# Stick-breaking attention on one core: products in two 64-row tiles throughout, and projection groups as a stream of halves

## The chip, the cores and the metric

The kernel runs on one core of a Trainium2 chip. The metric is the device time of one execution in microseconds, as the median of several runs. The input is one sequence of 2048 tokens with 1024 columns, all in float32.

## The reference

With DEPTH = 1 only the first kind of layer runs, the stick-breaking attention. Cut to what matters:

```python
h = rmsnorm(x, a_norm)
q, k, v, g = split(h @ w_in, 4)              # 16 heads of 64
for each head, t, s < t:
    z = (q[t] . k[s]) / 8
    log_beta, log_rem = log_sigmoid(z), log_sigmoid(-z)
    w[t, s] = exp(log_beta + sum of log_rem[t, j] over s < j < t)
o[t] = sum over s of w[t, s] * v[s]
out = rmsnorm(x + (o * silu(g)) @ w_out, final_norm)
```

## The kernel before

The tokens are reversed on the host, so that the product over the keys between s and t becomes a running product along a row. The kernel never forms the weights w. ScalarE makes sigmoid(-z) of the scores (`stick`, L1161), VectorE multiplies it up along the row with a scan (`scan`, L1381), and since w is the difference of two neighbouring running products, the kernel multiplies the running product with differences of v (`dv_head`) instead.

Every product of two float32 matrices is made from three products of reduced float32 numbers, high part by high part, high by low and low by high. So each operand has a high part (a copy on ScalarE) and a low part (a subtraction on VectorE or GpSimd).

**Stages.** First v for all tokens (L817), then ten groups of the q, k and gate projection. Then the attention, with the rest of the projection spread through it, and at the end the output projection (L995), the residual and the last norm.

**Attention.** A step is 128 queries of one head against a chunk of 512 keys. Four steps are one slot, with 10 slots a head (4 on the diagonal, whose steps have 512, 384, 256 and 128 columns, and 6 full ones of 512 columns), 160 slots in all. In slot s TensorE makes, in the order in which it is written out:

- scores of slot s + 2 (L886): 12 products with 64 rows of contraction. Steps alternate between the upper and lower half of the array's rows, so two run beside one another.
- turns of slot s (L919, or L932): transposes of the running products, each as two 64-row halves into PSUM. ScalarE copies a pair of steps out as the high part (`hi`, L1166), and VectorE takes the low part (`lo`, L1385).
- one projection group (`project`, L864): 24 products of 256 columns on all 128 rows, in some slots two groups. A group is emptied by `made_high` on ScalarE and `made_low` on VectorE (L1365, L1367) and stored.
- weighings of slot s (`weigh`, L964 and L965): 8 products on 128 rows into the bank o_ps. At the end of a chunk of queries ScalarE empties that bank (`empty`, L1172) and the parts are stored.

The order of each engine is written out in a loop over the slots. `SLOT_GROUPS` says which slot has which groups, `LOAD_W`, `HI_W` and the `PAIR_` tables say at which step weights and differences of v are loaded and split. The turned parts have two places in PSUM, four banks in all (`turn_ps`), the scores three banks, whose free ones are lent to the groups.

## Time and profile before

| | us |
|---|---|
| median of 3 runs | 1605.23 |
| lowest and highest | 1601.46, 1605.66 |
| the profiled execution's own time | 1601.61 |
| its span, first to last instruction | 1599.9 |
| TensorE busy | 1577.8 |
| VectorE busy | 1281.8 |
| ScalarE busy | 848.4 |
| GpSimd busy | 423.5 |

A busy time is the union of an engine's instructions. Products on TensorE overlap, so its busy share says only that it had work; what a product costs is the distance between the starts of two that follow each other. The attention lasts from about 233 us to 1428 us.

### The profile page before, as it was taken

Reading aid. Unit: us, or ns where it says so; the run is one execution under the profiler, and the core shown is the slowest. Engines: PE = TensorE matmul, PEld = TensorE weight load, DVE = VectorE, ACT = ScalarE, POOL = GpSimd, SP = SyncE. Lnnn points to the kernel's source line nnn. Section 1 sums busy time; section 2 is a strip of 40 time slices with the busy share of each in tenths; the row PEclk is TensorE's granted clock in tenths of the full one; section 3 lists DMA queues with packets and bytes.
Section 4 is the critical chain, followed back from the end, with each engine's and each line's share of the span. In section 5 each row is a group of like instructions: output and inputs, shape, how many; then the busy total and the mean of one; then the engine's idle time right before and its main releaser. Section 6 shows DMA issues by size and latency. Waiting matters only on the chain.

```text
span 1599.9 us, 34375 instructions
## 1 busy us (share of the span) xinstructions
PE 1577.8 (99%) x13762; PEld 1382.1 (86%) x13762; DVE 1281.8 (80%) x1525; ACT 848.4 (53%) x1558; POOL 423.5 (26%) x520
## 2 busy tenths in 40 slices
PE   9999999999999999999999999999999999999998
PEld 7888888888898888888888888888888988778887
DVE  5445439898889898898989898889899888967883
ACT  6535335555555556556556565565556555752221
POOL 0022034223323243323432433233223432000000
PEclk9999999999999999999999999999999999999999
DMA  9868654443434252435343443424243433879632
GB/s 304 268 182 271 203 159 126 125 124 99 137 102 136 74 158 78 139 86 146 110 115 115 120 117 96 138 91 143 77 142 103 131 110 110 326 254 342 206 106 79
DMA packets 205887, 237.82 MB, mean 149 GB/s; under 512 B 54560, under 2 KB 162080, under 8 KB 205728
## 3 DMA queue, kind: packets, MB, share of 16 engines
q1 hardware_dynamic: 113344, 160.30, 32.7%
q10 hardware_dynamic: 92384, 75.33, 15.3%
q8 instruction: 109, 1.79, 0.5%
q14 instruction: 50, 0.41, 0.1%
HBM read 155.78 MB, written 79.76 MB: 147 GB/s over the span
## 4 chain that ended last, share of the span: by engine, by line
PE 84%; DVE 9%; ACT 3%; issue 2%; DMA 1%; SPq 0%; DVEq 0%; ACTq 0%
PE z_ps L864 29%; PE z_ps L886 12%; PE o_ps L965 6%; PE turn_ps L919 6%; PE o_ps L964 6%; DVE u L1381 5%; PE turn_ps L995 5%; PE z_ps L817 5%; PE z_ps L995 4%; DVE r_turned_lo L1385 3%; PE o_ps L817 3%; PE turn_ps L817 3%; PE turn_ps L864 1%; PE turn_ps L886 1%; PE o_ps L995 1%
## 5 line engine op out<-in xcount | busy, mean ns | idle before, releaser
L1381 DVE TENSOR_TENSOR_SCAN u<-u,u 128x512 f32<-128x512 f32 x384 | 500.0, 1337 | 0.0
L1161 ACT ACTIVATE u<-z_ps 128x512 f32<-128x512 f32 (+3 forms) x593 | 288.1, 541 | 302.2 <-PE z_ps L886 301.7
L864 PE MATMUL z_ps<-hT_hi,w_hi 128*128 128x256 f32 x1472 | 432.5, 294 | 2.9 <-ACT u L1161 2.1
L1385 DVE TENSOR_TENSOR r_turned_lo<-turn_ps,r_turned_hi 128x1024 fp32r<-128x1024 f32 (+1 forms) x320 | 324.0, 1053 | 129.5 <-ACT r_turned_hi L1166 128.3
L864 PE MATMUL z_ps<-hT_hi,w_lo 128*128 128x256 f32 x1472 | 416.0, 283 | 0.0
L864 PE MATMUL z_ps<-hT_lo,w_hi 128*128 128x256 f32 x1472 | 415.9, 283 | 0.0
L864 PEld LDWEIGHTS z_ps<-hT_hi,w_hi 128*128 128x128 f32 x1472 | 280.6, 191 | 28.9 <-issue 17.5
L864 PEld LDWEIGHTS z_ps<-hT_lo,w_hi 128*128 128x128 f32 x1472 | 281.3, 191 | 0.0
L864 PEld LDWEIGHTS z_ps<-hT_hi,w_lo 128*128 128x128 f32 x1472 | 281.2, 191 | 0.0
L1166 ACT ACTIVATE r_turned_hi<-turn_ps 128x1024 fp32r<-128x1024 f32 (+1 forms) x320 | 270.5, 905 | 6.6 <-PE turn_ps L919 6.6
L759 POOL TENSOR_SCALAR w_raw<-w_raw,a_norm_col 128x128 f32<-128x128 f32 x192 | 171.4, 909 | 241.5 <-DMA w_raw<-in_w_qkg 241.5
L964 PE MATMUL o_ps<-r_turned_hi,dv_head 128*128 128x512 f32 (+3 forms) x640 | 226.9, 359 | 0.0
L965 PE MATMUL o_ps<-r_turned_lo,dv_head 128*128 128x512 f32 (+3 forms) x640 | 223.9, 365 | 0.0
L1381 DVE TENSOR_TENSOR_SCAN u<-u,unbroken 128x512 f32<-128x512 f32 (+3 forms) x256 | 205.6, 843 | 2.7 <-ACT u L1161 2.7
L767 POOL TENSOR_TENSOR w_lo<-w_raw,w_hi 128x128 fp32r<-128x128 f32 x192 | 137.2, 745 | 215.1 <-ACT w_hi L1115 215.1
L886 PE MATMUL z_ps<-k_hi_twice,q_hi 64*128 64x512 f32 (+3 forms) x593 | 160.4, 441 | 8.9 <-issue 2.9
L919 PEld LDWEIGHTS turn_ps<-ident,u 64*128 64x128 f32 x4070 | 154.4, 139 | 13.2 <-DVE made L1367 0.5
L919 PE MATMUL turn_ps<-ident,u 64*128 64x64 f32 x4070 | 156.7, 223 | 0.0
L781 POOL TENSOR_TENSOR dv_head<-v_here,dv_head 128x256 fp32r<-128x256 f32 x64 | 53.8, 841 | 305.2 <-ACT dv_head L1109 305.2
L964 PEld LDWEIGHTS o_ps<-r_turned_hi,dv_head 128*128 128x128 f32 x640 | 120.8, 189 | 15.9 <-DVE r_turned_lo L1385 1.2
L965 PEld LDWEIGHTS o_ps<-r_turned_lo,dv_head 128*128 128x128 f32 x640 | 120.9, 189 | 15.5
L886 PE MATMUL z_ps<-k_hi_twice,q_lo 64*128 64x512 f32 (+3 forms) x593 | 133.3, 371 | 0.0
(157 smaller groups left out, 2220.9 us busy)
## 6 DMA issues: line engine op xcount, KB each, us to landing
qk_hi_cols<-made ACTq DMA_DIRECT2D x128, 128.0 KB, 2.3
qk_lo_cols<-made ACTq DMA_DIRECT2D x128, 128.0 KB, 2.3
k_hi_twice<-qk_hi_cols SPq DMA_DIRECT2D x128, 128.0 KB, 3.4
k_lo_twice<-qk_lo_cols SPq DMA_DIRECT2D x128, 128.0 KB, 3.7
x_T<-in_xT SPq DMA_DIRECT2D x29, 512.0 KB, 6.3
w_raw<-in_w_qkg SPq DMA_DIRECT2D x24, 512.0 KB, 3.8
x_rows<-in_x SPq DMA_DIRECT2D x16, 512.0 KB, 5.2
v_rows<-v_stage ACTq DMA_DIRECT2D x32, 256.0 KB
```

What stands on the lines that cost most here:

```text
L759: last = nc.gpsimd.tensor_scalar(w_raw[t % 2][:, k, :], w_raw[t % 2][:, k, :], norm_col[:, k:k + 1], None, ALU.mult)
L817: last = nc.tensor.matmul(v_ps[v % len(v_ps)][:], a[:, c, k, tok], b[:, k, :], start=(k == 0 and n == 0), stop=(k == KT - 1 and n == 2))
L864: last = nc.tensor.matmul(bank_of(g)[:, 0:GW], a[t % 2][:, k, :], b[:, c // 2, k, cols], start=(n == 0), stop=(n == QPM - 1))
L886: last = nc.tensor.matmul(score_bank(step), a[c % 2][rows, tau], b[rows, sig], start=(n == 0), stop=(n == 2))
L919: last = nc.tensor.transpose(turn_ps[p % 2][:, half, at:at + HALF], u_t[m // CB % RU][t][rows, r * P - lo:(r + 1) * P - lo], ident[rows, r ...
L964: nc.tensor.matmul(o_ps[:, 0:w], weights, rt_hi[p % 2][:, here], start=begin, stop=False)
L965: last = nc.tensor.matmul(o_ps[:, 0:w], weights, rt_lo[p % 2][:, here], start=False, stop=end)
L995: last = nc.tensor.matmul(y_banks(n)[f][:], a[t % RG][:, k, tok], b[:, k, f * CH:(f + 1) * CH], start=(m == 0), stop=(m == QPM - 1))
L1161: nc.scalar.activation(u_t[(m // CB) % RU][r][:, 0:w], score_bank(m), ACT.Sigmoid, scale=-Z_SCALE).then_inc(s_u, 1)
L1166: nc.scalar.activation(by_halves(rt_hi[p % 2][:], p), turned(p), ACT.Copy).then_inc(s_hi, 1)
L1381: nc.vector.tensor_tensor_scan(u, u, other, start, ALU.mult, op).then_inc(s_r, 1)
L1385: nc.vector.tensor_tensor(by_halves(rt_lo[p % 2][:], p), turned(p), by_halves(as_f32(rt_hi[p % 2][:]), p), ALU.subtract).then_inc(s_lo, 1)
```

## The change

All products of the attention work in 64-row tiles now. A weighing is split in two, over the upper and the lower 64 rows, and runs in one half of the array beside scores of a later slot in the other half (`weigh_beside`). The lower and the upper part of one pair of steps go one after the other into the same bank, with semaphores between them. The projection groups become a stream of halves: each of the 24 products of a group is an upper and a lower one, and the lower ones are at least 30 behind the upper ones, so that a group's lower half begins after its upper one has ended. `QUOTA` sets how many halves of each kind a half slot gets (12 on the diagonal, 15 else). Where a weighing takes more columns than the scores beside it, or fewer, group halves are put on the half with less.

The turned parts have one place in PSUM (two banks), and the turns of a pair of steps wait for the low part of the pair before. Scores have two banks, groups three. VectorE makes one scan, then the low part, then the other scan of a half slot; ScalarE's order is by half slots too. Separate forms of the turns beside scores (`turns_beside_scores`) are gone.

```diff
-SLOT_GROUPS = groups_of_slots()
+AHEAD = {-2: (BEFORE, BEFORE + 1), -1: (BEFORE + 2, BEFORE + 3)}
+FIRST = BEFORE + 4
+BEHIND = 30
+QUOTA = {True: 12, False: 15}
+STREAM = (NG - FIRST) * QPM
...
+def limits():
+    upto = [0]
+    for h in range(2 * NU):
+        _, c, j, _ = STEPS[CB * (h // 2)]
+        upto.append(min(upto[-1] + QUOTA[c == j], STREAM + BEHIND))
+    return upto
...
-        turn_ps = [ctx.enter_context(nc.psum_tensor(f"turn_ps{n}", [P, 2, CH], F32)) for n in range(2)]
-        t_ps = [turn_ps[n // 2][:, n % 2, :] for n in range(4)]
+        turn_ps = ctx.enter_context(nc.psum_tensor("turn_ps", [P, 2, CH], F32))
+        t_ps = [turn_ps[:, 0, :], turn_ps[:, 1, :], pb("group_ps0"), pb("group_ps1")]
+        g_ps = [z_ps[2], t_ps[2], t_ps[3]]
...
                 def turns(p):
 
+                    if p:
+                        pe.wait_ge(s_lo, p)
...
+                def group_half(low):
+                    i = made_so_far[low]
+                    made_so_far[low] += 1
+                    g, n = FIRST + i // QPM, i % QPM
+                    t, c = GROUPS[g]
+                    cols = slice(c % 2 * GW, (c % 2 + 1) * GW)
+                    if n == 0 and low:
+                        pe.wait_ge(s_gu, g - FIRST + 1)
+                    if n == 0 and not low:
+                        pe.wait_ge(s_plo, g - 2)
+                        if g == FIRST_G[t]:
+                            pe.wait_ge(s_wlo, t + 1)
+                    rows = slice(low * HALF, (low + 1) * HALF)
+                    k, (a, b) = n // 3, ((w_hi, hT_hi), (w_hi, hT_lo), (w_lo, hT_hi))[n % 3]
+                    last = nc.tensor.matmul(bank_of(g)[:, 0:GW], a[t % 2][rows, k, :], b[rows, c // 2, k, cols],
+                                            start=(n == 0 and not low), stop=(n == QPM - 1 and low == 1))
...
+                def left(h, low):
+                    limit = UPTO[h + 1] - BEHIND if low else UPTO[h + 1]
+                    return max(0, min(limit, STREAM) - made_so_far[low])
+
+                def group_pairs(h, share):
+                    both = min(left(h, 0), left(h, 1)) // share
+                    for _ in range(both):
+                        group_half(0)
+                        group_half(1)
+                    if share == 1:
+                        for low in range(2):
+                            for _ in range(left(h, low)):
+                                group_half(low)
+
+                def weigh_half(m, low, part):
...
+                    first = begin and not low and part == 0
+                    if first and NC * h + c:
+                        pe.wait_ge(s_ost, NC * h + c)
+                    rows = slice(low * HALF, (low + 1) * HALF)
+                    here = slice(blocks_before(m) * P, blocks_before(m) * P + w)
+                    turned_part = (rt_hi, rt_lo)[part]
+                    last = nc.tensor.matmul(o_ps[:, 0:w], dv_head[rows, j * CB + sigma_block(m), :], turned_part[p % 2][rows, here],
+                                            start=first, stop=(end and not low and part == 1))
...
+                def weigh_beside(p, low, m, h):
+                    weighed = inside(p // 2)
+                    scored = m < NS
+                    if weighed:
+                        pe.wait_ge(s_lo, p + 1)
+                        if p % 2 == 0 and low:
+                            pe.wait_ge(s_wu, p // 2 + 1)
+                        if p % 2 and not low:
+                            pe.wait_ge(s_wl, p // 2 + 1)
+                    for i in range(2 * PAIR):
+                        if weighed:
+                            weigh_half(PAIR * p + i // 2, low, i % 2)
+                        if scored and i < 3:
+                            score(m, i)
+                    width = 2 * (turn_width(PAIR * p) + turn_width(PAIR * p + 1)) if weighed else 0
+                    spare = width - (3 * (CH - score_cols(m)) if scored else 0)
+                    idle = low if spare < 0 else 1 - low
+                    for _ in range(min(abs(spare) // GW, left(h, idle))):
+                        group_half(idle)
...
+                for s in range(NU):
+                    ahead = CB * (s + LEAD)
+                    pe.wait_ge(s_r, CB * s + CB)
+                    turns(2 * s)
+                    weigh_beside(2 * s - 1, 1, ahead, 2 * s)
+                    group_pairs(2 * s, 2)
+                    weigh_beside(2 * s - 1, 0, ahead + 1, 2 * s)
+                    group_pairs(2 * s, 1)
+                    if s >= OUT_SLOT:
+                        put_out((s - OUT_SLOT) * QPM, (s - OUT_SLOT) * QPM + QPM // 2)
+                    turns(2 * s + 1)
+                    weigh_beside(2 * s, 0, ahead + 2, 2 * s + 1)
+                    group_pairs(2 * s + 1, 2)
+                    weigh_beside(2 * s, 1, ahead + 3, 2 * s + 1)
+                    group_pairs(2 * s + 1, 1)
...
@@ scalar
+                    for part in range(2):
+                        h, first = 2 * s + part, CB * s + PAIR * part
+                        for g in finished(h - 1):
+                            made_high(g)
+                            store_high(g)
+                        if inside(s):
+                            hi(h)
+                        for g in finished(h - 1):
+                            store_low(g)
+                        if inside(s + LEAD):
+                            stick(first + LEAD_SCORES)
+                            stick(first + LEAD_SCORES + 1)
...
+                        if ended is not None and part == 0:
+                            empty(ended)
+                        if ended is not None and part == 1:
+                            store_o(ended)
...
@@ vector
+                    for part in range(2):
+                        h, first = 2 * s + part, CB * s + PAIR * part
+                        for g in finished(h - 1):
+                            made_low(g)
+                        for m in range(first + LEAD_SCORES - PAIR, first + LEAD_SCORES):
+                            if 0 <= m < NS:
+                                scan(m)
+                            if inside(s) and m % PAIR == 0:
+                                lo(h)
```

## Rows read from the trace of the kernel before

**Rows 1.** The page: busy times, and the chain that ended last by engine.
```profile
PE 1577.8 (99%) x13762; PEld 1382.1 (86%) x13762; DVE 1281.8 (80%) x1525; ACT 848.4 (53%) x1558; POOL 423.5 (26%) x520
PE 84%; DVE 9%; ACT 3%; issue 2%; DMA 1%; SPq 0%; DVEq 0%; ACTq 0%
```

**Rows 2.** The chain of waits in order of time: start us, us, what; the double slots.
```profile
459.17 5.96 PE z_ps L864 x48
...
1350.85 5.95 PE z_ps L864 x48
```

**Rows 3.** Busy PE, PEld, DVE, ACT, POOL in these heads; granted clock, DMA share, GB/s.
```profile
459.17:1350.85 891.68, 887.91 (x8907) 789.61 (x8905) 795.34 (x856) 517.67 (x969) 309.64 (x368) 1.00 0.39 114
```

**Rows 4.** Timeline of TensorE, one full slot: start us, us, what, count.
```profile
702.19 0.39 PE L964 MATMUL o_ps<-r_turned_hi,dv_head 128*128 128x512 f32 x1
702.42 0.39 PE L965 MATMUL o_ps<-r_turned_lo,dv_head 128*128 128x512 f32 x1
702.74 0.50 PE L886 MATMUL z_ps<-k_hi_twice,q_hi 64*128 64x512 f32 x2
703.07 0.40 PE L886 MATMUL z_ps<-k_hi_twice,q_lo 64*128 64x512 f32 x2
...
703.54 1.16 PE L919 MATMUL turn_ps<-ident,u 64*128 64x64 f32 x32
704.51 0.48 PE L886 MATMUL z_ps<-k_hi_twice,q_hi 64*128 64x512 f32 x2
704.83 0.39 PE L886 MATMUL z_ps<-k_hi_twice,q_lo 64*128 64x512 f32 x2
...
705.39 0.39 PE L864 MATMUL z_ps<-hT_hi,w_hi 128*128 128x256 f32 x1
705.61 0.28 PE L864 MATMUL z_ps<-hT_lo,w_hi 128*128 128x256 f32 x1
705.73 0.28 PE L864 MATMUL z_ps<-hT_hi,w_lo 128*128 128x256 f32 x1
...
710.30 0.50 PE L886 MATMUL z_ps<-k_hi_twice,q_hi 64*128 64x512 f32 x2
```

**Rows 5.** The waits: engine and line, waited for, us in total, times, longest us.
```profile
PEld z_ps L886 <- issue: 43.7, 107, 3.3
```

**Rows 6.** Timeline of TensorE in diagonal scores of 256 and 128 columns.
```profile
696.12 0.54 PE L886 MATMUL z_ps<-k_hi_twice,q_hi 64*128 64x256 f32 x2
696.34 0.18 PEld L886 LDWEIGHTS z_ps<-k_hi_twice,q_hi 64*128 64x128 f32 x1 [0.20 <-PE z_ps L886]
696.34 0.43 PE L886 MATMUL z_ps<-k_hi_twice,q_lo 64*128 64x256 f32 x2
696.45 0.29 PEld L886 LDWEIGHTS z_ps<-k_lo_twice,q_hi 64*128 64x128 f32 x2
696.57 0.32 PE L886 MATMUL z_ps<-k_lo_twice,q_hi 64*128 64x256 f32 x2
```

**Rows 7.** Timeline of TensorE in diagonal weighings.
```profile
687.10 0.33 PE L964 MATMUL o_ps<-r_turned_hi,dv_head 128*128 128x384 f32 x1
687.27 0.34 PE L965 MATMUL o_ps<-r_turned_lo,dv_head 128*128 128x384 f32 x1
```

**Rows 8.** ScalarE: two instructions of its timeline, then groups by line (count, busy us, mean ns).
```profile
703.74 0.60 ACT L1161 ACTIVATE u<-z_ps 128x512 f32<-128x512 f32 x1 [2.35 <-PE z_ps L886]
704.23 0.59 ACT L1161 ACTIVATE u<-z_ps 128x512 f32<-128x512 f32 x1
L1166 ACT ACTIVATE r_turned_hi<-turn_ps 128x1024 fp32r<-128x1024 f32 x144 | 140.2, 1032 | 0.0
L1172 ACT ACTIVATE o_stage<-o_ps 128x512 f32<-128x512 f32 x48 | 30.1, 627 | 0.0
```

**Rows 9.** VectorE: the scans' spread (ns min/median/max), and the low parts by line.
```profile
L1381 DVE TENSOR_TENSOR_SCAN u<-u,u x384: 1248/1274/1821, 225.7 to 1406.6; 128x512 f32<-128x512 f32 x192
L1385 DVE TENSOR_TENSOR r_turned_lo<-turn_ps,r_turned_hi 128x1024 fp32r<-128x1024 f32 x144 | 169.2, 1216 | 75.0 <-ACT r_turned_hi L1166 74.1
```

More of the change, by code:

```diff
@@ L491, in lows_stored @@
                 eng.wait_ge(s_gst[parity], low_stores(g, parity))
[L493 to L498 removed]
         def score_bank(m):
[L502 to L507 removed]
+            return z_ps[m % 2][:, 0:CH - score_cols(m)]
         def bank_of(g):
@@ L866, in project, with score @@
                     last.then_inc(s_p, 1)
-                def scores(m):
-                    r = m % CB
-                    steps = (m + 1, m) if diagonal(m // CB) and r == 0 else (m, m + 1)
-                    for n in range(3):
-                        for step in steps:
-                            if diagonal(m // CB) and n == 0 and step % CB == CB - 1:
-                                pe.wait_ge(s_z, CB * (m // CB) + 1)
-                            score(step, n)
-                def score(step, n):
-                    _, c, j, r = STEPS[step]
+                def score(m, n):
+                    h, c, j, r = STEPS[m]
+                    if n == 0:
+                        if m >= 2:
+                            pe.wait_ge(s_u, m - 1)
+                        if r == 0 and c == 0:
+                            pe.wait_ge(s_k[j], 64 * (h + 1))
+                        if r == 0 and j == c:
+                            pe.wait_ge(s_q[c % 2], 64 * (2 * h + c // 2 + 1))
                     a, b = ((q_hi, k_hi), (q_lo, k_hi), (q_hi, k_lo))[n]
@@ L957, in weigh @@
-                    if begin and NC * h + c:
+                    first = begin and not low and part == 0
+                    if first and NC * h + c:
                         pe.wait_ge(s_ost, NC * h + c)
-                    p = m // PAIR
-                    if m % PAIR == 0:
-                        pe.wait_ge(s_lo, p + 1)
-                    here = slice(blocks_before(m) * P, blocks_before(m) * P + w)
-                    weights = dv_head[:, j * CB + sigma_block(m), :]
-                    nc.tensor.matmul(o_ps[:, 0:w], weights, rt_hi[p % 2][:, here], start=begin, stop=False)
@@ L965, in weigh @@
-                    last = nc.tensor.matmul(o_ps[:, 0:w], weights, rt_lo[p % 2][:, here], start=False, stop=end)
-                    if end:
-                        last.then_inc(s_o, 1)
-                    elif j == c and r == CB - 1:
-                        last.then_inc(s_dvused, 1)
+                    rows = slice(low * HALF, (low + 1) * HALF)
[3 more added lines that the diff above has]
+                                            start=first, stop=(end and not low and part == 1))
@@ new lines, in weigh_half @@
+                    if part == 1 and m % PAIR == 1:
+                        if p % 2 == 0 and not low:
+                            last.then_inc(s_wu, 1)
+                        elif p % 2 and low:
+                            last.then_inc(s_wl, 1)
+                        elif p % 2 and end:
+                            last.then_inc(s_o, 1)
+                        elif p % 2 and j == c:
+                            last.then_inc(s_dvused, 1)
+                def weigh_beside(p, low, m, h):
+                    weighed = inside(p // 2)
+                    scored = m < NS
+                    if weighed:
+                        pe.wait_ge(s_lo, p + 1)
+                        if p % 2 == 0 and low:
[12 more added lines that the diff above has]
+                        group_half(idle)
@@ L1277, in _ @@
-                    if inside(s + LEAD):
-                        stick(CB * (s + LEAD) + 2)
-                        stick(CB * (s + LEAD) + 3)
-                    if ended is not None:
-                        store_o(ended)
-                    for m in range(CB * s, CB * s + CB):
-                        if m in PAIR_HI:
-                            dv_hi(*PAIR_HI[m])
-                    for n, g in enumerate(SLOT_GROUPS.get(s, [])):
-                        if n:
-                            store_low(g - 1)
-                        made_high(g)
-                        store_high(g)
```

206 lines of the change are left out of this document (67 added, 139 removed).

## The prediction

> **What bounds the kernel now.** I read the page first: TensorE is busy 99% of the span, VectorE 80%, and the chain that ended last lies 84% on TensorE [rows 1]. The reader should not stop there, because a busy TensorE can be one that runs the wrong things slowly. So next the chain of waits in order of time, which gives the rhythm: two groups of projection in one slot (48 products in one row) recur once a head, and from 459.17 to 1350.85 are 12 heads, 74.3 us each [rows 2]. They hold 3 further double slots, so 11.25 groups (270 products of 256 columns) a head. The busy table over the same stretch says VectorE works 795 of 892 us, 66.3 us a head, and that TensorE has its full clock of 2.4 GHz (1.00) throughout [rows 3]. That is how much room there is: a head can't go below about 66 us, and TensorE must be the one that shortens it.
>
> Then the timeline of TensorE over one slot, whose starts tell what each thing costs [rows 4]. A slot whose weighings and scores are both full takes 7.56 us (702.74 to 710.30). Starts lie 0.12 us apart for a 256-column product on all 128 rows, 0.23 for a 512-column weighing, 0.235 for a pair of 512-column scores in the two row halves (two in 0.47, 703.07 to 703.54), and 0.030 for one 64-column turn (32 in 0.97 us, the halves taking turns, 0.061 a pair). Where the kind of tile changes there are steps longer than these: the last weighing before the scores takes 0.32 (0.09 over), the first scores 0.33 (0.10 over), the last scores before the group 0.33 (0.56 for two, 704.83 to 705.39, 0.09 over), the first product of the group 0.22 (0.10). The waits name them: 107 weight loads of scores come after idle time that no semaphore ended, some 0.35 us each as the weight loader counts it [rows 5]. The first scores after the turns take 0.32 too, with no change of tile: the wider weight load isn't hidden behind a 64-column product. That is 0.083 over.
>
> **The change, part by part.**
> *Switches removed.* With weighings and groups in 64-row tiles, a slot has no change of kind: minus 0.38 us of the slot above.
> *Exposed loads added.* Each of the two batches of turns is now followed by weighings and scores, so 0.083 twice a slot, 20 a head: 1.7 us.
> *Turns* stay: 32 in a full slot and 20 in a diagonal one, 6 and 4 slots a head, 272 x 0.0303 = 8.2 us.
> *Weighings beside scores.* Each of the 40 calls a head puts four weighings in one half and three scores in the other, then the spare column count in 256-column halves of groups on the half that has less. They are written W S W S W S W, then the group halves. What counts is whether a product can pass one written before it that waits for the other half. Rows 6 speak on that: at 696.12 a 256-column score is followed in its half by one that waits for nothing but its own half, free at 696.24, yet it starts at 696.34, when the other half's score written before it has been released by its semaphore (weight load, 0.20 idle). So program order holds across the halves, and I count with it: a product starts when its half is free and the one before it has started. The spare halves then start only with the fourth weighing. With 0.232 for 512 columns (between 0.229 and 0.235), 0.172 for 384 [rows 7], 0.11 for 128 (its load, which takes the 0.11 between two load starts [rows 6]) and 0.122 for 256, a call takes: full weighings beside scores of 512, 384, 256, 128 columns 0.94, 1.06, 1.31, 1.43 us (16, 2, 3, 3 of them; the last is 3 x 0.232 + 6 x 0.122); the first pair of a diagonal slot 0.82, 1.12, 1.25 (6, 1, 1, beside 512, 256, 128); its second pair 0.94 beside 512 (0.464 until the fourth weighing, 0.11, and three halves) and 0.59 beside 384 (6, 2). Sum 39.5 us a head. In them run 106 group halves, worth 53 full products.
> *Groups as halves.* 270 - 53 = 217 pairs a head. The trace has no pair of 256-column halves. Below it is bounded by the full product, 0.120 [rows 4], and by the one half seen alone in its lane, 0.12 from its load at 696.45 to its start at 696.57 [rows 6]. Above, I take 0.130: the aligned pair of 512-column scores costs 6 ns more than a full product, which I double. Nearest is the 0.12 plus a part of the 6 ns: 0.122. 217 x 0.122 = 26.5 us.
> Together 39.5 + 26.5 + 8.2 + 1.7 = 75.9 us against 74.3: plus 1.5 to 1.6, 25 us over 16 heads. The unmixed slot gains (0.97 + 0.17 + 4 x 0.94 + 20 x 0.122 = 7.3 for 24 products' worth, against 7.56), and the slots where full weighings meet diagonal scores, or diagonal ones meet full scores, give back more.
> On this order stands a rule of the Trainium skill (TensorE: Matmul & The Clock Gate, "The mechanism" in Part 3): products start in program order, whatever their tile, and only weight loads are pulled ahead. It speaks against the change, and the trace agrees with its 0.20 us of idle. The page TensorEngine Tiling (Array Packing), "Key Properties", has the opposite pull: a change of tiling mode drains the engine; by that alone the change would take 0.38 us off each of 160 slots, 61 us in all.
> *The end of a chunk.* The first weighing of a chunk waits for ScalarE to empty o_ps (L1172), and now only the end of one half slot lies between. From the start of the last score of that half slot: 0.39 until its end, 0.04 until ScalarE starts, 0.49 to its next start, 0.63 for the emptying [rows 8], 0.05 to release: 1.6 us. TensorE meanwhile has 0.47 of the call left, five pairs (0.61), six turns (0.18) and the exposed load: 1.3. Behind the waiting weight load stands everything, scores included. 0.3 us, 4 a head, 64 in all: 19 us. Bounds 0 (emptying first seen by TensorE just in time) and 0.5, 32 us. Before, a slot's scores, turns and group (5.6 us) covered it.
> *One turned bank instead of two.* Turns of one half slot wait for the low part of the last. After the turns: 0.2 to ScalarE, 1.03 for the high part, 1.22 for the low one [rows 8, 9], 2.5 us, inside a half slot of 3.6 to 4.1 us. VectorE puts one scan (1.34) ahead of the low part and one behind: 1.34 + 1.22 + 1.34, less 0.08 of overlap each (the next starts so much before the end), and 0.32 for a group in five of eight: 3.9 in a full half slot of TensorE's 4.0. I cost this at nothing: single long scans (up to 1.82) fit into the leeway of over 1 us that the turns' loop has. Without that leeway a long scan costs its 0.5 us, and the cost is rival C's.
> *The stream and its end.* Quotas of 15 and 12 pairs a half slot are 276 a head, 6 more than before, so the 4272 pairs run out in slot 155 instead of 157. Slots 156 and 157 have no group, 4.4 and 3.6 us on TensorE against 7.3 and 4.5 of scans and low parts: 4 us idle. Bounds 0 (the scans had run ahead) and 8. Groups' stores, high parts and weights keep their number; a group's bank is needed 18 pairs after its end, over a half slot, in which its low part is made at the head of VectorE's queue. SP's and POOL's orders keep their steps.
> Sum: 25 + 19 + 4 = 48 us slower than the profiled execution's own 1601.6: 1649 us. That execution stands 3.6 us below the median of 1605.2 and 0.15 above the lowest, so the sum may fall 2 to 3 us short of a median.
>
> **The rivals.**
> A. *The halves slip past each other.* If a group half may start while a weighing written before it waits, a call takes the longer of its two halves' sums: 35.9 instead of 39.5, the head 72.3, minus 2.0 x 16 = 32, and with 19 + 4: 1592, faster; with pairs at 0.120 and no chunk wait 1562. For it: neighbours in opposite halves start within 4 ns. Against it: rows 6. It decides from 1.4 us a head saved.
> B. *Feeding.* A pair is four instructions in 0.12 us. The turns show that rate, 32 in a batch [rows 4], which a queue may hold; over 892 us only 8907 products started, one in 0.10 us [rows 3], and the changed kernel wants about 120 in 8 us. If a product's load and start took 0.075 us when sustained, a pair would be 0.15: 270 x 0.028 = 7.6 a head, 1649 + 121 = 1770. For it: nothing stalls so in the trace. Against: batches at twice that rate.
> C. *VectorE becomes the bound* in full half slots, 3.9 against 4.0. If one in four of the 12 a head loses 0.3 us, that is 0.9 a head, 14 us: 1663 with the forecast (within its range), 1606 with A, no change. For it: 66.3 us a head and scans of 1.82 [rows 3, 9]; against it: the average head leaves it 9 us.
> D. *The chunks' ends wait for nothing*, because the turns before them are late anyway: 1649 - 19 = 1630, at the forecast's low end.
>
> **How the numbers follow.** Forecast with its pitches and waits between their bounds (1622 to 1691: pairs at 0.130 add 42) and D within it 0.66; A 0.20; C with A 0.04; B 0.10. Faster by over 0.3% (5 us, what a measurement here can tell): A and half of C, 0.22; within it 0.05; slower 0.73. Cutting off most of B above and a part of A below: 1582 to 1695; the forecast's own range is 1622 to 1691.
>
> **What would show it.** No idle of the weight loads of scores that no semaphore ends (switches gone); weighings 0.23 apart in one half with scores between them; pairs of group halves 0.122 apart; beside scores of 128 columns, the first spare group half starting with the fourth weighing (order holds) or right after the third score (A is right); waits of the first weighing of a chunk on the emptying, 64 of 0.3 us; a head at 77 us with VectorE busy 86% of it. The forecast is wrong if a head is under 74 us, or if the pair takes 0.115 or 0.14.

## The result, and the profile after

The changed kernel takes 1632.74 us (median of 4 runs, 1623.55 to 1634.36) against 1604.99 (4 runs): a ratio of 1.0166 (interval 1.0125 to 1.0207). It is slower. The profiled execution took 1633.79 us with a span of 1632.0, 32.2 us more than the profiled one of before.

The page: busy times, and the chain that ended last, as in [rows 1].
```profile
PE 1571.3 (96%) x19314; PEld 1458.5 (89%) x19314; DVE 1284.4 (79%) x1525; ACT 883.3 (54%) x1558; POOL 419.5 (26%) x520
PE 74%; DVE 7%; ACT 7%; issue 4%; DMA 3%; ACTq 2%; POOL 1%; SPq 1%; DVEq 0%
```
TensorE is busy for less time than before (1571.3 against 1577.8 us) in a longer span, and its share of the last chain falls from 84% to 74%, while ScalarE's rises from 3% to 7%. So the loss is mostly time in which TensorE waits, and ScalarE has a part in it. TensorE's waits over the whole span (line, waited for, us in total, times, longest us) name two; L902 are the turns, L957 the weighings:
```profile
PE turn_ps L902 <- DVE r_turned_lo L1404: 30.1, 50, 1.8
PE o_ps L957 <- ACT o_stage L1190: 16.3, 46, 3.3
```
The row of [rows 5] has no counterpart: the idle of the scores' weight loads at a change of tile is gone. The second wait is the forecast's emptying at the end of a chunk. The first, turns that wait for the low part of the half slot before, the forecast costed at nothing.

Busy PE, PEld, DVE, ACT, POOL by stretch, then granted clock, DMA share and GB/s: the start of the attention, the 12 heads of [rows 3], and the last head.
```profile
233.00:300.00 67.00, 64.67 (x917) 61.95 (x919) 58.62 (x61) 38.36 (x68) 22.85 (x30) 0.95 0.38 114
459.00:1350.00 891.00, 861.13 (x13031) 832.60 (x13028) 784.30 (x844) 536.04 (x956) 305.41 (x367) 1.00 0.40 114
1350.00:1460.00 110.00, 98.50 (x1132) 85.18 (x1129) 86.15 (x102) 68.19 (x132) 2.19 (x3) 0.94 0.67 224
```
In the 12 heads TensorE now idles 30 of 891 us, where it idled 4 of 892 [rows 3]; 29.2 of the 30 are the two waits (18.2 and 11.0 us there). A head, from one last emptying to the next, takes 75.41 us instead of 74.29 (mean of the 3rd to the 14th, called the steady ones), with 276 pairs of group halves in it and not 270. The last head takes 89.2 us instead of 78.3, and the clock falls to 1.2 GHz in it for two stretches of about 7 us each (from 1373.9 and 1435.3 on).

The 32 us, by the times of the first turn and of the last emptyings: the attention begins 3.3 us earlier; the 15 heads before the last take 26.2 more (the 12 steady ones 12 x 1.12 = 13.4; the others 12.8, of which 7.6 in the very first, 3.1 in the second and 2.0 in the 15th); the last head 10.9 more; what follows it 1.8 less.

How the halves run, from TensorE's timeline (start us, us, what, count): first the pairs of group halves at the end of a call.
```profile
764.30 0.33 PE L923 MATMUL group_ps<-hT_hi,w_hi 64*128 64x256 f32 x2
764.42 0.32 PE L923 MATMUL group_ps<-hT_lo,w_hi 64*128 64x256 f32 x2
764.54 0.33 PE L923 MATMUL group_ps<-hT_hi,w_lo 64*128 64x256 f32 x2
764.65 0.33 PE L923 MATMUL group_ps<-hT_hi,w_hi 64*128 64x256 f32 x2
```
Pairs of group halves start 0.12 us apart (0.117 over 764.30 to 764.65): just under the 0.122 of the forecast. Then a call whose diagonal weighings (256, 256, 128 and 128 columns) stand beside scores of 512 columns:
```profile
766.67 0.28 PE L957 MATMUL o_ps<-r_turned_hi,dv_head 64*128 64x256 f32 x1
766.72 0.28 PE L923 MATMUL group_ps<-hT_hi,w_hi 64*128 64x256 f32 x1
766.79 0.28 PE L957 MATMUL o_ps<-r_turned_lo,dv_head 64*128 64x256 f32 x1
766.84 0.39 PE L880 MATMUL z_ps<-k_hi_twice,q_hi 64*128 64x512 f32 x1
766.91 0.22 PE L957 MATMUL o_ps<-r_turned_hi,dv_head 64*128 64x128 f32 x1
766.97 0.27 PE L957 MATMUL o_ps<-r_turned_lo,dv_head 64*128 64x128 f32 x1
767.08 0.33 PE L923 MATMUL group_ps<-hT_lo,w_hi 64*128 64x256 f32 x1
767.08 0.39 PE L880 MATMUL z_ps<-k_hi_twice,q_lo 64*128 64x512 f32 x1
...
767.31 0.39 PE L880 MATMUL z_ps<-k_lo_twice,q_hi 64*128 64x512 f32 x1
```
They are written W S W S W S W. The fourth weighing starts at 766.97, before the second score (767.08) and the third (767.31), both written ahead of it. In all 124 calls of the trace with such weighings beside scores of 512 or 384 columns the fourth weighing starts before a score written ahead of it, by 0.03 to 0.37 us. Products of one half pass products of the other: rival A's mechanism, which the forecast had ruled out.

One of the new waits, on ScalarE's timeline (ACTq rows are DMAs that its queue issues; L1179 brings a score bank over, L1144 is the high part of a finished group, L1184 the high part of the turned halves). The turns of this half slot started at 447.38 and ended by 448.07.
```profile
446.96 0.28 ACT L1179 ACTIVATE u<-z_ps 128x128 f32<-128x128 f32 x1 [0.93 <-PE z_ps L880]
446.97 0.48 ACTq L1196 DMA_DIRECT2D o_hi_cols<-o_stage  x1
447.49 0.62 ACTq L1197 DMA_DIRECT2D o_lo_cols<-o_stage  x1
448.31 0.39 ACT L1144 ACTIVATE made<-z_ps 128x256 fp32r<-128x256 f32 x1 [1.07 <-PE z_ps L923]
448.72 0.32 ACTq L1156 DMA_DIRECT2D qk_hi_cols<-made  x1
449.09 1.03 ACT L1184 ACTIVATE r_turned_hi<-turn_ps 128x1024 fp32r<-128x1024 f32 x1 [0.40 <-ACT made L1144]
```
The high part starts 1.0 us after its turns are done, behind the output's two DMA issues, the group's high part and that group's store. VectorE and then TensorE follow, each late:
```profile
450.15 1.23 DVE L1404 TENSOR_TENSOR r_turned_lo<-turn_ps,r_turned_hi 128x1024 fp32r<-128x1024 f32 x1 [0.40 <-ACT r_turned_hi L1184]
451.43 0.65 PE L902 MATMUL turn_ps<-ident,u 64*128 64x64 f32 x14 [0.40 <-DVE r_turned_lo L1404]
```
VectorE was idle for 0.40 before its low part, so it was not VectorE's amount of work that made this one late. Counted over the trace, 10 of the 50 waits (6.5 of the 30.1 us) are of this kind. In 30 others (18.7 us) ScalarE's lateness takes a longer way: the low part of a finished group stands at the head of VectorE's half slot and, in 29 of them, is what waits for ScalarE; a scan follows, and then the turned low part. One of these, whose turns had ended by 803.8, and for which ScalarE first issued an output store until 803.58 and copied weights from 803.63:
```profile
804.60 0.36 ACT L1142 ACTIVATE made<-z_ps 128x256 f32<-128x256 f32 x1
804.86 1.02 ACT L1184 ACTIVATE r_turned_hi<-turn_ps 128x1024 fp32r<-128x1024 f32 x1
804.99 0.42 DVE L1384 TENSOR_TENSOR made<-z_ps,made 128x256 f32<-128x256 f32 x1 [1.57 <-ACT made L1142]
805.33 1.40 DVE L1400 TENSOR_TENSOR_SCAN u<-u,u 128x512 f32<-128x512 f32 x1
806.66 1.19 DVE L1404 TENSOR_TENSOR r_turned_lo<-turn_ps,r_turned_hi 128x1024 fp32r<-128x1024 f32 x1
807.90 0.71 PE L902 MATMUL turn_ps<-ident,u 64*128 64x64 f32 x16 [1.19 <-DVE r_turned_lo L1404]
```
The high part is done at 805.88 and lies there for 0.8 us. In the last 10 (4.9 us) VectorE did not idle so shortly before.

The waits sit at the same places. Of the 18.2 us in the 891 us, 15.9 (26 of 32 times) are at four of a head's 20 half slots, and all four come one half slot after one for which ScalarE has, ahead of the group and the high part, the two DMA issues of a chunk's output. Without the waits themselves, half of the half slots ahead of a wait last 3.3 to 3.7 us, where the forecast counted with 3.6 to 4.1.

### The profile page after: what moved, and what is told of

It is laid out like the page before. It is cut to its first block, busy times and chain, and to the rows that moved or that the text cites. A ratio compares the mean times of both kernels' runs of the same rounds, so it can differ in the third digit from the quotient of the medians.

```text
span 1632.0 us, 46030 instructions
## 1 busy us (share of the span) xinstructions
PE 1571.3 (96%) x19314; PEld 1458.5 (89%) x19314; DVE 1284.4 (79%) x1525; ACT 883.3 (54%) x1558; POOL 419.5 (26%) x520
## 4 chain that ended last, share of the span: by engine, by line
PE 74%; DVE 7%; ACT 7%; issue 4%; DMA 3%; ACTq 2%; POOL 1%; SPq 1%; DVEq 0%
PE o_ps L957 14%; PE group_ps L923 14%; PE z_ps L880 10%; PE z_ps L923 7%; PE turn_ps L902 7%; PE z_ps L814 5%; PE z_ps L1014 4%; DVE r_turned_lo L1404 4%; DVE u L1400 3%; PE o_ps L814 3%; PE group_ps L814 3%; PE turn_ps L1014 3%; PE group_ps L1014 2%; ACT o_stage L1190 2%; ACT u L1179 2%
## 5 line engine op out<-in xcount | busy, mean ns | idle before, releaser
L957 PE MATMUL o_ps<-r_turned_hi,dv_head 64*128 64x512 f32 (+3 forms) x1280 | 482.4, 381 | 18.0 <-ACT o_stage L1190 16.3
L1179 ACT ACTIVATE u<-z_ps 128x512 f32<-128x512 f32 (+3 forms) x640 | 336.2, 532 | 251.7 <-PE z_ps L880 241.1
L957 PE MATMUL o_ps<-r_turned_lo,dv_head 64*128 64x512 f32 (+3 forms) x1280 | 454.5, 365 | 0.0
L923 PE MATMUL group_ps<-hT_hi,w_hi 64*128 64x256 f32 x1888 | 451.7, 281 | 0.0
L923 PE MATMUL group_ps<-hT_hi,w_lo 64*128 64x256 f32 x1888 | 449.0, 280 | 0.0
L923 PE MATMUL group_ps<-hT_lo,w_hi 64*128 64x256 f32 x1888 | 446.9, 279 | 0.0
L1184 ACT ACTIVATE r_turned_hi<-turn_ps 128x1024 fp32r<-128x1024 f32 (+1 forms) x320 | 287.7, 899 | 185.8 <-PE turn_ps L902 165.5
L923 PEld LDWEIGHTS group_ps<-hT_hi,w_hi 64*128 64x128 f32 x1888 | 318.8, 186 | 3.1
L923 PEld LDWEIGHTS group_ps<-hT_lo,w_hi 64*128 64x128 f32 x1888 | 315.3, 186 | 2.1
L923 PEld LDWEIGHTS group_ps<-hT_hi,w_lo 64*128 64x128 f32 x1888 | 314.5, 186 | 1.0
L923 PE MATMUL z_ps<-hT_hi,w_hi 64*128 64x256 f32 x960 | 269.9, 281 | 0.0
L923 PE MATMUL z_ps<-hT_hi,w_lo 64*128 64x256 f32 x960 | 269.1, 280 | 0.0
L957 PEld LDWEIGHTS o_ps<-r_turned_hi,dv_head 64*128 64x128 f32 x1280 | 241.0, 188 | 31.2 <-issue 26.8
L957 PEld LDWEIGHTS o_ps<-r_turned_lo,dv_head 64*128 64x128 f32 x1280 | 240.5, 188 | 4.3
L902 PE MATMUL turn_ps<-ident,u 64*128 64x64 f32 x4352 | 205.1, 224 | 31.0 <-DVE r_turned_lo L1404 30.1
```

The lines of the kernel that those rows point to most:

```text
L902: last = nc.tensor.transpose(turn_ps[:, half, at:at + HALF], u_t[m // CB % RU][t][rows, r * P - lo:(r + 1) * P - lo], ident[rows, rows])
L923: last = nc.tensor.matmul(bank_of(g)[:, 0:GW], a[t % 2][rows, k, :], b[rows, c // 2, k, cols], start=(n == 0 and not low), stop=(n == QPM ...
L957: last = nc.tensor.matmul(o_ps[:, 0:w], dv_head[rows, j * CB + sigma_block(m), :], turned_part[p % 2][rows, here], start=first, stop=(end ...
L1179: nc.scalar.activation(u_t[(m // CB) % RU][r][:, 0:w], score_bank(m), ACT.Sigmoid, scale=-Z_SCALE).then_inc(s_u, 1)
L1184: nc.scalar.activation(by_halves(rt_hi[p % 2][:], p), turned(p), ACT.Copy).then_inc(s_hi, 1)
```

## The experiments

All stand beside runs of the kernel before on the same chip (medians 1604.5, 1604.8, 1604.9 and 1604.3 us in the four sets); ratios are to those, with their intervals. The changed kernel itself ran again in the first set only; the others are read beside that run, called the base. Line numbers shift by a few where an edit adds lines.

**The changed kernel again**, as the base of the first set.

> The changed kernel itself, once more, beside which the others are read. Both theories: 1633 us within 6, TensorE waits of 1.6 us a head for the low part and 0.9 us a head for the emptying of o_ps, and a few stretches at the half clock.

1627.38 us (5 runs, 1626.99 to 1632.6), 1.0156 (1.0141 to 1.0171). A steady head takes 75.29 us, of which 1.4 are waits for the low part and 0.9 for the emptying. The same picture, but the first head takes 79.0 us, not 84.6, and up to the attention's end 17.1 us of the trace are at 1.2 GHz, not 27.3. So some 5 us lie between two runs of one kernel. Over the whole span TensorE waits for the low part 48 times, 27.9 us, and for the emptying 46 times, 16.6 us.

**Is it the order across halves?** The spare group halves are spread between the weighings instead of standing behind them.
```diff
                     for i in range(2 * PAIR):
...
+                        for _ in range((i + 1) * extra // 4 - i * extra // 4):
+                            group_half(idle)
```


> In each call the spare group halves are written between the weighings and scores, evenly, instead of after the fourth weighing; nothing else. Theory O (my prediction: a product never starts before one written ahead of it, also in the other half) says the calls shrink from 39.5 to about 36 us a head, 55 us less in all: some 1580 us. Theory S (a product starts as soon as its own half is free, and passes what is written before it for the other half) says no change: 1633 us within 6, and in the trace of the changed kernel fourth weighings that start before third scores written ahead of them.

1636.98 us (1632.27 to 1640.16), 1.0199 (1.018 to 1.0218): 10 us slower than the base, where the order theory wanted 55 less. With the timeline above this settles it: the spare halves were not being held back by program order, so nothing could be won by writing them elsewhere. Why it is slower stays open; the two waits take 31.5 us of its 891, where they take 27.4 in the base, and its trace has 30.7 us at 1.2 GHz to the base's 17.1.

**The emptying, one place earlier** on ScalarE: before the second score bank of the half slot, not behind it.
```diff
                         if inside(s + LEAD):
                             stick(first + LEAD_SCORES)
+                        if ended is not None and part == 0:
+                            empty(ended)
+                        if inside(s + LEAD):
                             stick(first + LEAD_SCORES + 1)
```


> ScalarE empties o_ps at the end of a chunk before the second score step of that half slot, not after it. If the wait for the emptying sets the time, its 16 us in 46 waits go nearly to 0 (the emptying comes 0.49 us sooner, the waits are 0.35 on average) and the kernel takes 1618 to 1622 us. If those waits cover another one (the low part for the turns before it is late anyway), the time stays at 1633 and waits for the low part grow by as much.

1622.41 us (1619.23 to 1627.81), 1.0112 (1.0096 to 1.0128), 5 less than the base. A head is 0.56 us shorter. The waits of this kernel:
```profile
PE turn_ps L902 <- DVE r_turned_lo L1405: 33.0, 56, 2.1
PE o_ps L957 <- ACT o_stage L1190: 4.0, 2, 3.5
```
16.6 us of waiting for the emptying became 4.0, 3.5 of it in the last head, and 5.1 us came back as waits for the low part: part of one wait had covered the other.

**The high part ahead of the finished group** on ScalarE, and the low part ahead of the group's on VectorE. The store of the group's low part moves too, behind ScalarE's two score banks.
```diff
+                        if inside(s):
+                            hi(h)
                         for g in finished(h - 1):
                             made_high(g)
                             store_high(g)
-                        if inside(s):
-                            hi(h)
-                        for g in finished(h - 1):
-                            store_low(g)
                         if inside(s + LEAD):
                             stick(first + LEAD_SCORES)
                             stick(first + LEAD_SCORES + 1)
+                        for g in finished(h - 1):
+                            store_low(g)
...
@@ vector
-                        for g in finished(h - 1):
-                            made_low(g)
...
                             if inside(s) and m % PAIR == 0:
                                 lo(h)
+                            if m % PAIR == 0:
+                                for g in finished(h - 1):
+                                    made_low(g)
```


> In each half slot ScalarE makes the turned high part before the group's high part and its store, and VectorE makes the group's low part after the turned low part. Theory Q (the turns wait because ScalarE starts the high part 0.8 to 2.2 us late, behind a group's emptying and DMA issues in its queue): the 30 us of waits for the low part fall to under 8 us, the time to about 1608. Theory V (they wait because VectorE has no room: two scans and a low part take 3.9 us in half slots in which TensorE needs 3.5): the waits stay above 20 us and the time at 1628 or more, since VectorE has the same work.

1672.83 us (1669.02 to 1674.54), 1.0421 (1.0407 to 1.0436). TensorE's waits over the same 12 heads, first of the changed kernel, then of this one:
```profile
PE turn_ps L902 <- DVE r_turned_lo L1404: 18.2, 32, 1.7
PE o_ps L957 <- ACT o_stage L1190: 11.0, 36, 1.4
```
```profile
PE o_ps L957 <- ACT o_stage L1190: 18.8, 44, 1.3
PE group_ps L923 <- DVE made L1386: 9.4, 11, 1.4
PE turn_ps L902 <- DVE r_turned_lo L1404: 8.6, 12, 1.5
PE group_ps L923 <- DVE made L1384: 6.3, 7, 1.4
PE z_ps L923 <- DVE made L1386: 5.8, 8, 1.3
PE z_ps L923 <- DVE made L1384: 2.2, 3, 1.0
```
Slower by 45 us than the base, where theory Q had 1608; theory V's 1628 or more was to go with unchanged waits. The wait it aimed at halves (18.2 to 8.6 us), so what stands ahead of the two turned parts has a share in it; as both engines' orders were changed, the run does not say which. And 23.7 us of waits for the groups' banks take its place, since a bank is wanted 18 pairs, little more than a half slot, after its group ends.

**What a change of tile costs.** One extra 64-column product ahead of each of the 320 batches of turns, on 128 rows (two changes of tile a time), or on 64 rows (none).
```diff
+                    nc.tensor.matmul(turn_ps[:, 0, 0:HALF], ident[0:128, :], ident[0:128, 0:HALF], start=True, stop=True)
```


> Ahead of the turns of each of the 320 half slots one more product of 64 columns on all 128 rows is put in (identity by identity, into the bank that the turns then overwrite): a change of tile kind and back, 640 changes. Its neighbour has the same product on 64 rows. Both theories price a change of kind at about 0.19 us there and back (0.38 for two there and backs in the full slot of the kernel before): this one takes 60 us longer than its neighbour. If a change costs only what the exposed weight load costs, which both have, the two are equal within 6.

> The same product on 64 rows, so with no change of tile kind: 1627 us plus 320 small products, each with its exposed load, 0.1 to 0.2 us: 1660 to 1690.

With 128 rows 1737.36 us (1734.37 to 1741.13), 1.0826 (1.0806 to 1.0845); with 64 rows 1661.5 (1658.88 to 1662.22), 1.0349 (1.0333 to 1.0364). The same number of products, 75.9 us apart: 0.237 us for the way there and back, 0.24 by the heads too (82.15 against 77.34 us, for 20). The longer half slots also swallow waits: in the 12 steady heads TensorE idles 5.2 us with 128 rows and 15.7 with 64. With that counted in, its own work is 0.28 us longer each time. That the product itself has 128 rows, and its weights too, is not separated from the change of tile. The 64-row product alone costs 29 to 34 us, 0.1 each.

**VectorE's room.** Full steps scan the first 256 of their 512 columns only.
```diff
+                    if j != c:
+                        u, other = u[:, 0:CH // 2], other[:, 0:CH // 2]
```


> VectorE scans only the first 256 of 512 columns in the full steps (the running product of the other columns is left out), 0.6 us less in each of 384 scans, 15 us of work a head; nothing else changes. Theory V (VectorE's room sets the waits for the low part): those 25 to 30 us of waits vanish, time about 1600. Theory Q (ScalarE's late start sets them): in the waits that I looked at, VectorE took up the low part 0.03 to 0.25 us after the high part in half of them and 0.6 to 1.3 us after it in the others: about half goes, 1612 to 1618 us.

1616.58 us (1615.12 to 1616.66), 1.0069 (1.0057 to 1.0082). VectorE's busy time in the 891 us falls from 784 to 650 us, and TensorE's waits of the whole span read:
```profile
PE turn_ps L902 <- DVE r_turned_lo L1406: 22.4, 38, 1.4
PE o_ps L957 <- ACT o_stage L1190: 20.5, 53, 3.9
```
With 15% of VectorE's time handed back, 22.4 of the base's 27.9 us of low-part waits remain, and in 27 of the 38 VectorE was idle just before the low part, waiting for the high one. So VectorE's work is a part of the cause and, of these waits, the smaller one. In time the run is 10.8 us faster than the base, the most that any single edit brought; only some of that is in these waits, and where the rest is was not followed up.

**Another share of groups**, 13 pairs in a half slot with diagonal steps and 14 in the others (12 and 15 before), to lengthen the short half slots.
```diff
-QUOTA = {True: 12, False: 15}
+QUOTA = {True: 13, False: 14}
```


> 13 and 14 pairs a half slot instead of 12 and 15: 272 a head instead of 276, so the stream lasts two slots longer, and short half slots get more of it. Theory S with VectorE near its limit: the end of the last head (89 us against 75 for the others) gives back 5 to 8 us, while full half slots fall from 3.95 to 3.83 us, below VectorE's 3.9, which costs about as much: 1620 to 1630. By my prediction's sum alone (TensorE's work is the same, and the idle slots cost 4 us) it is 4 us faster.

1632.04 us (1629.52 to 1632.94), 1.0164 (1.0149 to 1.018): no gain, against an expected 1620 to 1630. Low-part waits are 34.9 us, those for the emptying 8.7, and the last head is 91.4 us (89.2 in the base), where a stream that lasts longer was expected to give back 5 to 8.

**The finished group's store behind the high part**, its making left where it is; then the same with the early emptying, and both with the quotas.
```diff
                         for g in finished(h - 1):
                             made_high(g)
-                            store_high(g)
                         if inside(s):
                             hi(h)
                         for g in finished(h - 1):
+                            store_high(g)
                             store_low(g)
```


> ScalarE issues the store of a group's high part after the turned high part instead of before it (0.33 to 0.4 us of waiting and issuing leaves the way in half slots that have a group's end); VectorE's order is as in the changed kernel, and the group's banks come free as soon. Theory Q: the waits for the low part shrink from 25 to about 15 us, the time to 1615 to 1620. Theory V: no change, 1627 to 1633.

> Both reorderings of ScalarE's queue, the store after the turned high part and the emptying ahead of the second score step. If the two waits are independent, their gains add: about 1610. Still not below the kernel before (1605), because 15 us of waits for the low part and the stretches at half clock stay.

> Both reorderings, and 13 and 14 pairs a half slot. With the low part coming sooner the even quotas should no longer cost a wait in full half slots, so that the longer stream shows: 2 to 6 us below the two reorderings alone. If VectorE's room is what is left (full half slots at 3.9 us), it is equal or a little slower.

Alone: 1628.55 us (1622.4 to 1630.41), 1.0135 (1.0119 to 1.0151). The time is the base's (1627.38) within the noise, as theory V had it (1627 to 1633) and not theory Q (1615 to 1620). The 12 steady heads take 4.8 us less, but the first head takes 4.8 more, with a stretch at 1.2 GHz that the base has not (27.3 us in all, 17.1 in the base), and the last 3.5 more. Low-part waits fall only from the base's 27.9 to 26.0 us, though in half of them the high part now starts within 0.5 us of the turns' end (0.94 in the base). The rows from 804.60 on say why: the group's high part still stands behind the output's issues, and 34 of the 46 waits come by way of the group's low part and the scan behind it on VectorE (28 of 48 in the base). The earlier turned high part is not what these wait for. With the early emptying 1619.48 us (1613.79 to 1620.35), 1.0086 (1.0072 to 1.01), a head at 74.49: 3 us under the early emptying alone, and not the 1610 of two gains that add. With the quotas too 1623.29 us (1614.05 to 1626.1), 1.0107 (1.0088 to 1.0127): no help, and 41.0 us at 1.2 GHz.

**The output's DMA issues moved as well.** For the three chunks a head whose next slot ends no chunk, the two issues of L1196 and L1197 go behind the next high part; with the two edits above.
```diff
+                        if kept is not None and part == 0:
+                            store_o(kept)
+                            kept = None
...
                         if ended is not None and part == 1:
-                            store_o(ended)
+                            if s >= NU - 2 or chunk_end(s) is not None:
+                                store_o(ended)
+                            else:
+                                kept = ended
```


> As store_after_empty_early, and ScalarE's two DMA issues for a chunk's result (0.5 and 0.6 us of its queue) move from the end of the half slot to behind the next turned high part, for the three chunks a head whose next slot ends no chunk. Theory Q: the half slots with most of the waits for the low part follow just these issues (slots 1, 5 and 8 of a head), so 15 of the 25 us go and the time is 1600 to 1606, level with the kernel before or a little below. Theory V (VectorE's room): the waits in these half slots stay, 1616 to 1620.

1611.49 us (6 runs, 1607.77 to 1617.5), 1.0039 (1.0025 to 1.0054): the fastest variant, 1.2% under the change as it was made, and still 0.4% slower than the kernel before. A steady head takes 74.17 us, less than the 74.29 of before and with six more pairs in it. In the 891 us these waits are left (the profiled execution was the slowest of the six, 1617.5 us):
```profile
PE turn_ps L902 <- DVE r_turned_lo L1412: 11.2, 20, 2.3
PE o_ps L957 <- ACT o_stage L1190: 2.6, 2, 1.9
```
The time lies between the two theories (1600 to 1606, and 1616 to 1620). At the four places, beside the run with the two reorderings alone, two are nearly gone (3.2 and 3.1 us of waits there become 0.2 and 0.7), the third keeps its 2.3, and the fourth, whose output store was not moved, keeps 3.8 of 4.2. That confirms the output's DMA issues in ScalarE's queue as the cause at these two places; at the third it does not. The other waits, the last head (89 to 94 us in these kernels) and the stretches at 1.2 GHz stay.

## Why the prediction was right, and where it was not

It said slower, 1649 us with 1582 to 1695, and the kernel is slower by 28 us, not 44. The direction and the range hold, but the direction by luck: without its waits a head would be 1.3 us shorter than before, where the forecast had it 1.6 longer, and what makes the kernel slower is mostly a wait that the forecast costed at nothing. The sum came near by two errors of opposite sign.

**The step that failed** is "program order holds across the halves". It made the calls 39.5 us a head; slipping, they are 35.9. Taking the waits out of the measured head (18.6 and 10.5 us in the 12 steady ones) leaves 75.41 - 1.55 - 0.88 = 73.0 us for 276 pairs, 72.3 for 270 (6 x 0.118 less). The forecast's own work was 75.9, rival A's 72.3. In [rows 6] a product with nothing to wait for stood behind one of the other half that waited for a semaphore. That such a wait holds back what is written behind it is true (a row under the chunk's end below shows it again); that a half busy with its products does so as well was read into it. The trace of after has 124 calls that contradict it. By the rule of the Trainium skill (TensorE: Matmul & The Clock Gate, "The mechanism" in Part 3) products start in program order; across two row halves the trace disagrees, by up to 0.37 us, for products that wait for no semaphore.

**The step that took its place** is the cost of the one turned bank: nothing forecast, 30.1 us in 50 waits measured, some 1.6 us a head. The forecast summed the chain as 0.2 + 1.03 + 1.22 = 2.5 us inside a half slot of 3.6 to 4.1. Two terms were wrong. ScalarE does not start 0.2 us after the turns but 0.8 us or more in 35 of the 50 waits, because DMA issues of 0.32 to 0.62 us each and a group's high part are queued ahead; the forecast counted the group for VectorE (0.32) but nothing for ScalarE's queue. In 29 of the 50 the same queue held up VectorE too, by the finished group whose low part VectorE makes first, and a scan then stands ahead of the turned low part. The room shrank as well: without the order across halves, the half slots ahead of the waits mostly last 3.3 to 3.7 us. output_store_late took the waits away at two places by clearing that queue; store_after, which left the group's high part behind the output's issues, took only 1.9 us of them; short_scans shows rival C, the scans, as a part, with 5.5 of 27.9 us. Most of the rest of the 27.9 no run has removed without another wait in its place.

**Switches.** A full slot was to lose 0.38 us, for two rounds between tiles. switch_in against switch_out gives 0.24 for one round in time, 0.28 in TensorE's own work; the forecast had 0.19. The Trainium skill (TensorEngine Tiling (Array Packing), "Key Properties") says that a change of tiling mode drains the engine: the runs agree with a price of that size, though they don't show what TensorE does in it. The exposed load after the turns is there as forecast: full products start at 758.26, their followers at 758.58, 0.08 over 0.235.

**Pairs of halves** at 0.117 to 0.120 us instead of 0.122; rival B, feeding, is out: 13031 products ran in 891 us.

**The chunk's end** cost 16.3 us in 46 waits, forecast 19 in 64. One of them, and the first score written behind it, which waits for no one but starts only with it:
```profile
762.00 0.47 PE L957 MATMUL o_ps<-r_turned_hi,dv_head 64*128 64x512 f32 x1 [0.25 <-ACT o_stage L1190]
...
762.00 0.49 PE L880 MATMUL z_ps<-k_hi_twice,q_hi 64*128 64x512 f32 x1
```
Rival D, by which this wait comes to nothing behind late turns, did not come as such, but the overlap that it names is there: empty_early removes 12.6 us of this wait for 5 us of time.

**The end of the stream** was given 4 us. The last head is 10.9 us longer, with 5.6 us of waits for the low part, 3.5 for the emptying and two stretches at 1.2 GHz. That six pairs a head had run earlier, so that nothing was left to cover these waits, is a guess that quota_13_14 speaks against: with 272 pairs a head its last head takes 91.4 us. The cause stays open, and so does that of the 7.6 us in the first head.

**Rival A as a time** (1592) did not come: its head of 72.3 came out once the waits are taken off, but 2.4 us of waits a head, the first and the last head and the clock took it back.

**The clock**, which the forecast took as full throughout. Rows of before show 1.2 GHz nowhere in the attention; after has five stretches of it, 27.3 us in all. Two of them, each with the 4 us ahead of it (columns as above):
```profile
311.80:315.80 4.00, 2.21 (x34) 1.99 (x33) 3.28 (x4) 2.96 (x6) 2.07 (x3) 1.00 0.45 140
315.80:319.20 3.40, 3.40 (x26) 3.28 (x24) 3.39 (x4) 0.90 (x2) 3.40 (x3) 0.50 0.00 0
...
1066.10:1070.10 4.00, 2.29 (x35) 2.04 (x34) 3.35 (x4) 2.97 (x6) 1.24 (x3) 1.00 0.34 99
1070.10:1073.50 3.40, 3.40 (x28) 3.11 (x26) 3.31 (x4) 0.89 (x2) 0.00 (x0) 0.50 0.00 0
```
Ahead of both TensorE worked for 2.2 to 2.3 of 4 us, and idled for the rest in one wait of the turns for the low part, the two longest of that kind:
```profile
315.17 0.40 PE L902 MATMUL turn_ps<-ident,u 64*128 64x64 f32 x6 [1.79 <-DVE r_turned_lo L1404]
...
1069.45 0.40 PE L902 MATMUL turn_ps<-ident,u 64*128 64x64 f32 x6 [1.71 <-DVE r_turned_lo L1404]
```
In the 4 us ahead of the other three stretches it worked for 1.9 (first turns, 233.9), 1.7 (1373.9) and 3.2 us (1435.3). So a wait of 1.7 us can cost up to 1.7 more, the half of the 3.4 at 1.2 GHz that follow. It does not always: the base and store_after have one of 1.72 and 1.71 us at the same place (1065.0 and 1065.3 there), and the clock stays at 2.4 GHz behind both. All five stretches hold at most 13.7 us of the 32. That idle time brings the low clock on fits all five, but no run changed the clock alone, and the third set's missing gain (27.3 us at 1.2 GHz in store_after, 41.0 with the quotas) fits it only as a count.

## What to carry to other kernels

When two engines' handover gets less slack, list everything in the queue of the engine in between, DMA issues included, ahead of the instruction that now matters; here the waits behind that list (30.1 us) took back more than the change had won in TensorE's work (1.3 us a head). Look for the second way too: an instruction that is late in one queue holds up the next engine's queue by whatever stands at its head, and clearing the way of one instruction alone (store_after) brings little. Moving the turned parts ahead of the finished groups only traded one bank's waits for another's; more slack for each bank is the untried way. And judge an ordering rule by rows in which nothing waits for a semaphore.

## What the runs showed of the hardware that was not expected

- Two 64-row halves run as two streams. A product starts before products written earlier for the other half, by 0.03 to 0.37 us in 124 of 124 calls of one kind; a product that waits for a semaphore holds back those behind it in either half (the score that starts at 762.00 with the weighing written ahead of it, after its 0.25 us of waiting).
- A change between 64-row and 128-row products costs 0.237 us there and back (75.9 us for 320), 0.28 with the waits that it hides; the price of the one product's 128 rows is in it.
- Two loads and two products of 256 columns take 0.12 us (0.117 from 764.30 to 764.65), and nothing slows over a long time: 13031 products of all kinds in 891 us, the waits included.
- An issue of a DMA holds ScalarE's queue for 0.32 to 0.62 us, and the compute behind it waits that long (the turned high part at 449.09 started 1.02 us after its turns, behind four such entries).
- One wait of TensorE of 1.71 or 1.79 us was followed within 0.7 us by 3.4 us at 1.2 GHz; waits of 1.72 and 1.71 us in two other runs were not.
